# A hybrid attention and linear-recurrence block: seven block products in a second tile, with the weight sums made by accumulating DMAs

## What is computed

```python
h = rmsnorm(x, w_norm_pre)
proj = h @ w_in                                   # 1024 -> 3328
q_a, k_a, v_a, z_a, q_r, f_r, i_r, z_r = split(proj)
o_a = sliding_window_sink_attention(rope(q_a), rope(k_a), v_a, sinks) * silu(z_a)
o_r = rmsnorm(hgrn2_chunkwise(q_r, f_r, i_r, lb), hgrn_norm) * silu(z_r)
y = concatenate([o_a, o_r]) @ w_out               # 1024 -> 1024
x = x + rmsnorm(y, w_norm_post)
```

## Time and profile before

| | us |
|---|---|
| median of 3 runs | 865.83 (864.93 to 865.89) |
| the profiled execution | 864.57 |
| its span | 862.7 |

### The profile page before, as it was taken

How to read it: one execution, slowest core, us unless ns; L and a number is a source line. 1 busy time by engine, 2 the same in 40 slices (tenths; PEclk the granted TensorE clock), 3 DMA queues, 4 the chain that set the end, 5 groups by cost and what they waited for, 6 DMA issues and landing times.

```text
span 862.7 us, 12445 instructions
## 1 busy us (share of the span) xinstructions
PE 851.9 (99%) x4428; PEld 700.6 (81%) x4428; DVE 631.9 (73%) x1125; ACT 519.0 (60%) x1033; POOL 114.6 (13%) x84
## 2 busy tenths in 40 slices
PE   8999999999999999999999999999999999999997
PEld 6787788888888778888888878888888887888885
DVE  6878878674656799767747789887775368888846
ACT  7766445763466458567446655865853755576544
POOL 0000013430200000332020000144300000004220
PEclk9999999999999999999999999999999999999999
DMA  8686755748986647464898785445699674444586
GB/s 322 212 325 221 244 205 170 285 147 314 418 342 248 213 145 265 152 210 133 321 382 348 276 330 172 146 151 216 241 374 396 228 273 147 147 147 158 189 326 254
DMA packets 59981, 211.20 MB, mean 245 GB/s; under 512 B 6672, under 2 KB 6928, under 8 KB 59920
## 3 DMA queue, kind: packets, MB, share of 16 engines
q1 hardware_dynamic: 57904, 205.56, 65.3%
q10 hardware_dynamic: 2016, 4.85, 1.4%
HBM read 157.95 MB, written 52.43 MB: 244 GB/s over the span
## 4 chain that ended last, share of the span: by engine, by line
PE 84%; DVE 9%; ACT 4%; issue 3%; DVEq 0%
PE bank L596 55%; PE bank L605 5%; PE turn_b L852 3%; PE score_b L852 3%; PE bank L852 3%; PE score_b L605 3%; PE turn_b L605 3%; PE turn_b L653 2%; DVE kv_tok L1386 2%; PE score_b L629 2%; PE turn_b L706 2%; PE bank L697 1%; PE bank L687 1%; PE turn_b L709 1%; ACT probs_t L951 1%
## 5 line engine op out<-in xcount | busy, mean ns | idle before, releaser
L596 PE MATMUL bank<-h_hi,w_lo 128*128 128x512 f32 x832 | 326.9, 393 | 0.0
L596 PE MATMUL bank<-h_lo,w_hi 128*128 128x512 f32 x832 | 326.3, 392 | 0.0
L596 PE MATMUL bank<-h_hi,w_hi 128*128 128x512 f32 x832 | 324.4, 391 | 0.5 <-issue 0.5
L596 PEld LDWEIGHTS bank<-h_lo,w_hi 128*128 128x128 f32 x832 | 156.4, 188 | 34.7 <-issue 3.3
L596 PEld LDWEIGHTS bank<-h_hi,w_hi 128*128 128x128 f32 x832 | 156.4, 188 | 33.1 <-issue 1.0
L596 PEld LDWEIGHTS bank<-h_hi,w_lo 128*128 128x128 f32 x832 | 156.3, 188 | 32.8
L1716 POOL TENSOR_TENSOR mix_lo<-v_r,mix_hi 128x512 fp32r<-128x512 f32 x16 | 21.2, 1322 | 539.0 <-ACT v_r L1142 539.0
L1263 DVE TENSOR_TENSOR w_lo<-w_raw,w_hi 128x1024 fp32r<-128x1024 f32 x36 | 44.8, 1248 | 34.6 <-ACT w_hi L924 34.1
L1386 DVE STREAM_TRANSPOSE kv_tok<-k_mid 32x128 f32<-32x128 f32 x192 | 58.1, 303 | 2.8
L924 ACT ACTIVATE w_hi<-w_raw 128x1024 fp32r<-128x1024 f32 x38 | 39.8, 1051 | 24.9 <-issue 10.2
L1700 POOL TENSOR_TENSOR x_acc<-x_acc,x_sq 128x512 f32<-128x512 f32 x21 | 32.7, 1557 | 70.0 <-ACT x_sq L974 70.0
(11 more groups left out here) (280 smaller groups left out, 1549.2 us busy)
## 6 DMA issues: line engine op xcount, KB each, us to landing
w_hi<-kept_hi SPq DMA_DIRECT2D x108, 512.0 KB, 3.8
w_lo<-kept_lo SPq DMA_DIRECT2D x108, 512.0 KB, 4.9
w_raw<-in_weights SPq DMA_DIRECT2D x46, 512.0 KB, 6.2
kept_hi<-w_hi SPq DMA_DIRECT2D x34, 512.0 KB, 6.3
kept_lo<-w_lo SPq DMA_DIRECT2D x34, 512.0 KB, 7.4
x_in<-in_x_rows SPq DMA_DIRECT2D x8, 1024.0 KB, 8.1
x_in<-in_x SPq DMA_DIRECT2D x15, 512.0 KB, 6.6
kept_lo<-w_raw SPq DMA_DIRECT2D x8, 512.0 KB, 7.0
```

The lines of the kernel that those rows point to most:

```text
L596: mm = pe.matmul(acc(w)[:, :], stationary[:, s, k, :], moving[:, k, :], start=(m == 0), stop=(m == 3 * KT - 1), skip_group_check=True)
```

## The change

Tile 1 becomes a fast tile too (`FAST = 1`). The raw sums are no longer formed by DVE: GpSimd issues eight DMAs from DRAM to DRAM into a new tensor t_rows, four plain and four that add to what is there. Since these only add, two blocks keep the other sign, and `sum_head` and `post` turn it with a scalar_tensor_tensor instead of a tensor_tensor. In tile 1, one piece a step in steps 3 to 10, ACT rounds the sum's high half, DVE subtracts for the low half, and GpSimd issues the two saves. SP loads the pieces (`load_sum`). The buffers of pieces 2 and 3 are those of `probs` and `probs_t`, so DVE waits for their saves (`probs_saved`) ahead of the first softmax write of tile 1. GpSimd also issues the stores of tile 0, which ACT issued.

```diff
-FAST = 2
+FAST = 1
-SUMS_IN = (FAST - 1, H0 + 8), (FAST, 5)
-SUMS_OUT = ((FAST, 0, 0), (FAST, 1, 2)), ((FAST, H0, 0), (FAST, H0 + 2, 2))
-SUMS_AT = 5
+SUMS_IN = {(FAST - 1, OUT0): (0, 1), (FAST, 5): (2,), (FAST, 6): (3,), (FAST, 7): (4,), (FAST, 8): (5,), (FAST, 9): (6,), (FAST, 10): (7,)}
+SUMS_SPLIT = {3 + k: (k,) for k in range(T_TILES)}
...
+            def load_sum(k):
+
+                if k == 0:
+                    sp.wait_ge(t_made, 64)
...
+                sp.dma_start(t_in[k], t_rows[k * P:(k + 1) * P, :].rearrange("p (k m) -> p k m", k=KT)).then_inc(t_loaded[k], 16)
...
+            def sum_high(k):
+
+                act.wait_ge(t_loaded[k], 16)
+                act.activation(t_hi[k], t_in[k].rearrange("p k m -> p (k m)").rearrange("p (k n) -> p k n", k=2), ACT.Copy).then_inc(t_high, 1)
...
-                    for b, cols, pieces, pool_pieces in PLAIN_STORES if t < FAST else ():
-
-                        act.wait_ge(finished.sem, finished.after(t, pieces - 1))
...
+                if t == FAST and q == 0:
+                    dve.wait_ge(probs_saved, 64)
...
-                dve.tensor_tensor(s_tmp[:, S2, :], h_mix[:, 2 * P:], s3[:, h, :], ALU.subtract).then_inc(s_step, 1)
-                dve.tensor_tensor(s_tmp[:, S1, :], h_mix[:, 2 * P:], a21[:, h, :], ALU.add)
+                dve.scalar_tensor_tensor(s_tmp[:, S2, :], h_mix[:, 2 * P:], -1.0, s3[:, h, :], ALU.mult, ALU.subtract).then_inc(s_step, 1)
+                dve.tensor_tensor(s_tmp[:, S1, :], h_mix[:, 2 * P:], a21[:, h, :], ALU.subtract)
...
+            def sum_low(k):
+
+                dve.wait_ge(t_high, k + 1)
+                dve.tensor_tensor(t_in[k], t_in[k], t_hi[k].rearrange("p k n -> p (k n)").rearrange("p (k m) -> p k m", m=P), ALU.subtract).then_inc(t_low, 1)
...
+                if half:
+                    dve.scalar_tensor_tensor(dst, src, -1.0, w_post_t[:, half, :], ALU.mult, ALU.mult).then_inc(y_posted.sem, 1)
...
+            def save_sum(k):
+
+                pool.wait_ge(t_low, k + 1)
+                rows, saved = slice((WT + k) * P, (WT + k + 1) * P), probs_saved if k in (2, 3) else t_saved
+                pool.dma_start(kept[0][rows, :].rearrange("p (k m) -> p k m", k=2), t_hi[k].bitcast(FP32)).then_inc(saved, 16)
+                pool.dma_start(kept[1][rows, :].rearrange("p (k m) -> p k m", k=KT), t_in[k]).then_inc(saved, 16)
...
-            pool.wait_ge(lo_split.sem, lo_split.after(0, 3))
+            pool.wait_ge(lo_split.sem, lo_split.after(0, 6))
+
+            def sum_start(dst, src):
+                pool.dma_start(t_rows[dst * 2 * P:(dst + 1) * 2 * P, :], src).then_inc(t_base, 16)
+
+            def sum_add(dst, src):
+                pool.dma_start(t_rows[dst * 2 * P:(dst + 1) * 2 * P, :], src, accum_op=ALU.add, max_dma_last_dim=4 * KT * P).then_inc(t_made, 16)
...
+                    for k in SUMS_SPLIT.get(s, ()) if t == FAST else ():
+                        save_sum(k)
...
+                for b, cols, pieces, pool_pieces in PLAIN_STORES:
...
+                    pool.dma_start(out[bass.ds(t * N + b * P, P), cols[0] * N:(cols[-1] + 1) * N].rearrange("p (h n) -> p h n", n=N),
```

More of the change, by code:

```diff
@@ L50 @@
 OUT0 = H0 + 4 * HEADS
+LATE = 6
 WT = OUT0 + KT
@@ L304, in hybrid_block @@
         res_loaded = sem("res_loaded")
-        stored = [sem(f"stored{i}") for i in range(2)]
+        stored, pool_stored = ([sem(f"{n}{i}") for i in range(2)] for n in ("stored", "pool_stored"))
         def count(name, per_tile):
@@ L470, in load_split @@
                                  rows[row * P:(row + 1) * P, :].rearrange("p (k m) -> p k m", k=KT)).then_inc(w_ready[slot], 16)
[L472 to L488, removed]
+            def load_sum(k):
+                if k == 0:
+                    sp.wait_ge(t_made, 64)
+                if k == 2:
+                    sp.wait_ge(weighed.sem, weighed.after(FAST - 1, PAIRS - 1))
+                    sp.wait_ge(head_mixed.sem, head_mixed.after(FAST - 1, HEADS - 1))
+                if k >= 4:
+                    sp.wait_ge(lo_split.sem, lo_split.after(0, 0) + FRESH - RAW_SLOTS + k - 4)
+                sp.dma_start(t_in[k], t_rows[k * P:(k + 1) * P, :].rearrange("p (k m) -> p k m", k=KT)).then_inc(t_loaded[k], 16)
             def store_y(t, stores):
@@ L566, in _ @@
             store_y(TILES - 1, LAST_STORES)
-            sp.wait_ge(stored[0], 32 * TILES + 48)
-            sp.wait_ge(stored[1], 48 * TILES + 32)
+            sp.wait_ge(stored[0], 32 * (TILES - FAST) + 48)
+            sp.wait_ge(stored[1], 48 * (TILES - FAST) + 32)
+            for i in range(2):
+                sp.wait_ge(pool_stored[i], (32, 48)[i])
         @block.tensor
@@ L1140, in _ @@
                             act.wait_ge(o_done.sem, o_done.after(t, head))
+                            if t == FAST and head == 0:
+                                act.wait_ge(probs_saved, 64)
                             act.activation(o_sq_hi, out_b, ACT.Square)
@@ L1185, in _ @@
                             square_y(t, 0, b)
-                        for k in range(4) if t == FAST - 1 else ():
-                            sums_high(k)
                 if t < FAST:
@@ L1650, in _ @@
                             sum_head(t, h)
-                    if t == FAST and 0 <= s - SUMS_AT < 4:
-                        sum_weights(1, s - SUMS_AT)
+                    for k in SUMS_SPLIT.get(s, ()) if t == FAST else ():
+                        sum_low(k)
                     for i in splits(t, s) if (t, s) != (1, 0) and (t or kind not in (0, 1)) else ():
@@ L1660, in _ @@
                         dve.tensor_scalar(y_bias[:, :], y_sq[:, 0:4], 1.0 / D_MODEL, EPS, ALU.mult, ALU.add).then_inc(y_biased.sem, 1)
-                        for part in range(4) if t == FAST - 1 else ():
-                            sum_weights(0, part)
                 if t >= FAST:
```

101 lines of the change are left out of this document (50 added, 51 removed).

## The result

The changed kernel takes 867.62 us (median of 8, 866.69 to 870.24), the kernel before 865.51 beside it: a ratio of 1.0029 (95% interval 1.0018 to 1.0041; ratios here are taken over whole sets of runs and can differ a little from the quotient of two medians). So it is slower by some 2 us, where the forecast was 863.4, faster by 2.4. The time lies above the forecast's own range (861.7 to 864.7), and 0.1 us above the upper end of the wide one (860.6 to 867.5). The span of the profiled execution is 865.4 us, where it was 862.7.

What follows compares the result with a forecast made beforehand. PE was taken as the bound, busy 851.9 of 862.7 us; -4.6 - 0.2 + 2.1 + 0.3 = -2.4 us from the median 865.83 gave 863.4 us, range 861.7 to 864.7 (wide: 860.6 to 867.5).

Steps and rivals of the forecast that it cites:

- The fast form: Tile 1 on PE: 24 matmuls fewer, 5.44 us, less 0.8 of late starts; net -4.6 us.
- Tile 2's relief: Step 10 of tile 2: DVE's and ACT's work for the sums leaves, so the 0.23 us late start goes; -0.2 us.
- The halves' +2.1: Tile 1, step 10: DVE's and ACT's time for the sums' halves makes `weigh` start late; +2.1 us on PE, once.
- The chain from DRAM to DRAM: GpSimd's eight DMAs in tile 0: 86 us, done at 119, 8 us in time; cost 0.
- the middle price of 17.9: Assumed us per MB for an adding DMA in tile 0, the middle between 8.1 and 27.6.
- The third rival: Tile 0: slow adding DMAs hold GpSimd and PE stands still some 19 us; about 882 us, chance 0.15.
- a wait for probs_saved: Tile 1, step 8: DVE waits for piece 3's saves before writing `probs`; 0 to 3.3 us, taken as 0.3.
- a sign of being wrong: Among the stated signs: PE idling for weights in steps 7 to 12 of tile 1; no size given.
- the second rival: Tile 1: DMA queues full, piece 3's saves and weight pairs late; 866.4, up to 867.5 us, chance 0.18.

Runs made afterwards that it cites:

- the second profile: The changed kernel, unedited, run and profiled once more beside other kernels on one chip: 867.02 us, 1.0029 to the kernel before.
- the last order: Changed kernel with halves in steps 3, 4, 6 to 11, low ones on GpSimd from step 7, saves in steps 8 to 15: 860.93 us, 0.9959.
- the run without the late saves: Changed kernel with the saves of pieces 4 to 7 left out: 868.27 us, 1.0043 to the kernel before.

## Why the prediction was wrong

**The sum's terms held, but for one.** Not every one of them shows in the changed kernel itself, where PE's late weights cover the halves; the runs bring them out one by one. The fast form: -4.6 forecast, -4.5 by the stretch of tile 1 without saves and halves (209.0 for 213.5). Tile 2's relief: -0.2 forecast, -0.3 measured. The halves' +2.1: without the saves, gate_scale of step 10 came at 287.1 where the working has 287.2, ACT's copy 2.70 behind it, and `weigh` 2.0 late. The steps on the way agree too: gate_scale of steps 7 to 10 is late by 1.0, 2.2, 2.8 and 4.0 us, where the working has 0.6, 1.9, 2.7 and 4.1. The chain from DRAM to DRAM: no wait; GpSimd was through the fifth landing at 98 where the working had 119. Two copies side by side took 11.6 us, single ones 8.5; two adds side by side 21.4, single ones 13.0 and 13.3. So the middle price of 17.9 was too high, and the Trainium skill's half of a copy's rate ("Collectives: The Full Stack", section "The bandwidth ceiling: the fold count and why AG ≠ RS ≠ AR") is near for the pair (1.84 times a copy's time) and too much for a single one (1.55 times); the page states it for the rings of collectives. The third rival is out.

**The step that failed is what the full DMA queues cost.** The sum priced it at 0.3, as a wait for probs_saved, and let the weight pairs land in time, at no cost. The wait for probs_saved did not come in the changed kernel: DVE's write stands at 280.71, the saves landed at 277.3, since PE was late by then. On the working's clock, with the write at 275.4, it would have been 1.9 us and not 0.3, and with the stores on ACT it was 2.06. What came in its place are late weight pairs in steps 7 and 8, which the working names itself as a sign of being wrong. They stand in the second rival, and its price was wrong too: at most 1.1 us on top of the 3.3 (867.5 in all), where tile 1 lost 7.1 us. Put in the sum for +2.1 and +0.3, which it covers, it gives -4.6 - 0.2 + 7.1 = +2.3 by the profiled execution (+0.2 by the second profile, where 5.0 were lost); the medians differ by 867.62 - 865.51 = +2.1.

**Why the price was wrong.** The rival's text had the two numbers that decide: 289 GB/s added to 292, against 412 that the engines give. It then took the longest landing seen in a full queue (13.8 us) as the worst. But that queue emptied: the window of 412 GB/s is followed by one of 292. In the changed kernel more is asked for several steps than is moved, and what is left over adds up. An estimate from these numbers: 581 GB/s times a step of 5.44 us are 3.16 MB, and 412 move 2.24 MB of it, so after each such step a new DMA lands 0.92 MB / 412 GB/s = 2.2 us later than after the one before. Measured, the low halves of four pairs in a row, from step 7's on, landed in 13.1, 16.8, 18.1 and 20.7 us. The rival also took the pairs as issued three steps, 16.3 us, ahead of their use; SP's rows of the kernel before have 12.5 us for step 7 (252.35 to 264.82) and 15.4 for step 8, which leaves reserves of 4.9 and 7.2 us. Two or three steps use those up. By this working the second rival deserved far more than 0.18.

**What else no term had.** SP issued the pair of step 7 2.6 us late because earlier saves had not landed. That alone does no harm: without the sums' saves it was issued at 256.94 (255.2 on the scale of the kernel before), in the last order at 254.16, and both times it landed in time. And PE, once it had stood, had the lower clock for part of step 8, 1.7 us in one of two profiles.

## What to carry to other kernels

Add up the bytes that a change puts into each step and compare them with what the DMA engines move there at their fullest: where the sum is greater for several steps, the lateness grows, and the price is that of the backlog at the first transfer with a small reserve, not of one long landing. Take the reserve from the issue and landing rows, not from the program's order. Bytes that are needed late should be issued late: with the same 12.6 MB tile 1 lost 5 to 7 us when the saves went out as soon as they could, and nothing on the weights when they were held back by a few steps. When one cost falls on a stretch where another has already made PE late, as the halves' 2 us did here, the larger hides the smaller, and a run that leaves out only one of them does not show what each is worth.

## What the runs showed of the hardware

A DVE row with two SBUF operands, L1321, stood still while GpSimd worked on 1024 columns: 2.77 us for 0.69, three times; so did L1591 (2.88 for 0.68), and in the last order the scan L1627 (2.73 for 1.22). Rows on DVE that read a bank of PSUM beside such a GpSimd row kept their usual time (the reduction L1405 1.23 us, the same with and without). The Trainium skill, "SBUF — State Buffer", section "SBUF: two separate sides", describes such a pair of ports that the two engines take in turn for a whole instruction, and counts DVE operations with two SBUF inputs among those that need it; the trace agrees in these places. GpSimd takes 2.4 us for the subtraction for which DVE takes 1.23.

GpSimd's saves did not stand behind SP's loads: issued at 256.5 and 261.3, the high halves landed in 8.4 and 8.5 us (the low ones, issued right behind, in 10.3 and 10.5), while the pair that SP issued at 258.8 took 14.6 and 16.8. The Trainium skill, "DMA: Bandwidth & Descriptors", section "Queues, rings and completion order", has each DMA engine serve its queues in turn, packet by packet; by that, a queue with little in it overtakes a long one, and the trace agrees. GpSimd's transfers were thus not behind the weights but beside them.

The granted clock fell behind stands of PE in several profiles: to 0.66 over ten us after one of 7.2 us, to 0.86 after 3.2 and 1.8, to 0.83 after 2.8 and 1.7 (the run without the late saves). After 2.5 and 1.7 us it stayed at 1.00 in the changed kernel's second profile, and after the one of 1.9 in the run without saves.

In the first microseconds of some executions PE's matmuls came at an interval of 0.43 us until about 12 us, in others at 0.23 from 8.6 on, for the same program text at that place; the granted clock is listed as 1.00 in both, though 0.43 is the interval of the lower level. In the run without saves tile 1 then begins at 228.0, 1.7 us later than before. Where profiles are compared above, it is therefore by stretches of a tile and not by whole spans; the medians have this scatter in them.
